# A two-layer streaming encoder step on one core: values by channel, decays broadcast per token, another order of D's heads, an earlier first sum of squares

## What is computed

```python
h = rms(x, lp['norm_mix']); proj = h @ lp['w_in']
# group C, per head; dmat is a fixed causal decay
att = jnp.einsum('bihd,bjhd->bhij', qc, kc) * dmat
y = jnp.einsum('bhij,bjhe->bihe', att, vc) + jnp.einsum('bihd,bhde->bihe', qc, S) * cross
# group D, per head; bh are summed forget gates, igh input gates, m_t a running maximum
dm = jnp.where(tril, bh[..., :, None] - bh[..., None, :] + igh[..., None, :], -jnp.inf)
sc = jnp.einsum('bthd,bshd->bhts', qc, kc) * jnp.exp(dm - m_t[..., None])
num = jnp.einsum('bhts,bshe->bhte', sc, vc) + g[..., None] * jnp.einsum('bthd,bhed->bhte', qc, C)
# group B
q = rms(q_lat, lp['mla_q_norm']) @ lp['mla_wq_b']
kv = concat(past_ckv, ckv_new) @ lp['mla_wkv_b']
```

## Time and profile before

| | us |
|---|---|
| runs: median of 3 (least, most) | 972.83 (969.71, 972.98) |
| the profiled execution | 973.24 |
| its span, first to last instruction | 971.5 |
| TensorE busy with matmuls | 957.7 |
| VectorE, GpSimd, ScalarE busy | 505.5, 398.6, 201.1 |
| mean granted TensorE clock | 0.995 |

### The profile page before, as it was taken

How to read it: one execution, slowest core, us unless ns; L and a number is a source line. 1 busy time by engine, 2 the same in 40 slices (tenths; PEclk the granted TensorE clock), 3 DMA queues, 4 the chain that set the end, 5 groups by cost and what they waited for, 6 DMA issues and landing times. The chain is left out here.

```text
span 971.5 us, 15085 instructions
## 1 busy us (share of the span) xinstructions
PE 957.7 (99%) x5875; PEld 848.5 (87%) x5875; DVE 505.5 (52%) x989; ACT 201.1 (21%) x440; POOL 398.6 (41%) x386
## 2 busy tenths in 40 slices
PE   7999999999999999999999999999999999999998
PEld 6777887776999999999967678877779999999998
DVE  5464446773756556512253545568465665654321
ACT  3123233623000110100031142344320010001001
POOL 8000110033866666576301003001267666666770
PEclk9999999999999999999999999999999999999999
DMA  9932211117644554343433321121174554434421
GB/s 251 271 106 87 90 47 45 48 45 166 176 131 138 152 145 131 120 144 128 135 111 98 106 66 50 44 87 48 14 206 133 148 149 136 131 122 138 144 93 39
DMA packets 159043, 112.14 MB, mean 115 GB/s; under 512 B 10102, under 2 KB 156956, under 8 KB 158844
## 3 DMA queue, kind: packets, MB, share of 16 engines
q1 hardware_dynamic: 154388, 104.50, 37.3%
q0 software_dynamic: 3952, 5.92, 2.2%
q10 hardware_dynamic: 632, 0.75, 0.3%
HBM read 108.89 MB, written 2.27 MB: 114 GB/s over the span
## 5 line engine op out<-in xcount | busy, mean ns | idle before, releaser
L728 PE MATMUL ps<-hT,ring 128*128 128x320 f32 x576 | 164.3, 442 | 0.1
L728 PEld LDWEIGHTS ps<-hT,ring 128*128 128x128 f32 x576 | 109.5, 193 | 47.3 <-issue 3.8
L599 POOL TENSOR_TENSOR work<-ring 128x512 f32<-128x512 f32 (+1 forms) x66 | 82.5, 1250 | 153.3 <-issue 117.6
L1076 PE MATMUL ps<-mixT,ring 128*128 128x160 f32 x672 | 105.0, 299 | 0.0
L1076 PE MATMUL ps<-hT,ring 128*128 128x160 f32 x672 | 98.7, 300 | 1.3 <-DVE hT L1959 1.3
L1076 PE MATMUL ps<-hT,work 128*128 128x160 f32 x672 | 98.5, 299 | 0.0
L1076 PEld LDWEIGHTS ps<-mixT,ring 128*128 128x128 f32 x672 | 95.8, 190 | 0.0
L1076 PEld LDWEIGHTS ps<-hT,ring 128*128 128x128 f32 x672 | 93.7, 190 | 2.0 <-DVE hT L1959 1.5
L1076 PEld LDWEIGHTS ps<-hT,work 128*128 128x128 f32 x672 | 93.6, 190 | 0.1
L600 POOL TENSOR_TENSOR ring<-ring 128x512 f32<-128x512 f32 (+1 forms) x66 | 83.3, 1262 | 5.2
L601 POOL TENSOR_TENSOR work<-ring 128x512 f32<-128x512 f32 (+1 forms) x66 | 83.0, 1257 | 5.2
(11 more groups left out here) (380 smaller groups left out, 1466.1 us busy)
## 6 DMA issues: line engine op xcount, KB each, us to landing
ring<-in_w_gu SPq DMA_DIRECT2D x88, 512.0 KB, 5.2
ring<-in_w_in SPq DMA_DIRECT2D x44, 512.0 KB, 4.8
ring<-in_w_down SPq DMA_DIRECT2D x32, 512.0 KB, 4.5
ring<-in_w_out SPq DMA_DIRECT2D x16, 512.0 KB, 4.1
ring<-in_w_down SPq DMA_DIRECT2D x16, 384.0 KB, 3.7
cst<-in_consts POOLq DMA_DIRECT2D x1, 1664.0 KB, 11.9
ring<-in_w_in SPq DMA_DIRECT2D x2, 640.0 KB, 7.6
wqb<-in_mla_wq_b POOLq DMA_DIRECT2D x2, 384.0 KB, 7.6
```

Of the source, the lines that this page charges most:

```text
L599: step(tt(s3, a11, a21, ALU.subtract))
L728: ins = mm(bank(use, 0, T, m), w[:, k, c:c + m], hT[:, k, 0:T], start=(k == 0), stop=(k == KT - 1))
L1076: ins = mm(bank(use, at * HT, HT), left, right(k), start=(opens and k == 0 and at == 0), stop=(closes and k == n - 1), skip_group_check=True)
```

## The change

- The values of C and D are projected by channel with `feature`, two tiles of 128 channels each. ScalarE copies each to wt (columns 0 to 319 of two halves, `value_raw`), TensorE turns it in three transposes per tile (`value_tiles`), and ScalarE copies the result to vaug.
- The query squares of the two latent tiles are added by VectorE first, so that qms takes three products instead of six. Of gx, four products of one column become one of four columns, over a small diagonal that VectorE makes.
- dd is one product of all 320 columns; VectorE adds the mask in three pieces that pick the columns of the former layout.
- The order of D's heads: rq1, rk0 and rk1 come ahead of the scores and decays of the next head instead of behind them, and VectorE makes the next head's dmx after the weights of this one.
- Layer 0's first sum of squares: GpSimd's pair adds go; TensorE multiplies each square tile, the first three between the two halves of x's transposes. The cached latents move behind ql0 and ql1, on TensorE, ScalarE and VectorE.
- Layer 1: the squares and copies of ql0 and ql1 are interleaved with the key tiles.
- GpSimd's second weight mix of a layer waits for h_sums (before, the third did). Clears of wt cover columns 320 to 575 (before, 512 to 575).

```diff
@@ the dense uses of PSUM, two banks in turn
-    d(..., "mfg", "mv0", "mv1", "mv2")
-    u += [("cnT", (4,)), ("qms", (5,)), ("qt0", (6,)), ("qt1", (7,)), ("qt2", (2,))]
+    d(..., "mfg", "mv0", "mv1")
+    u += [("cnT", (4,)), ("qms", (5,))]
+    d("mvt0", "mvt1")
+    u += [("qt0", (6,)), ("qt1", (7,)), ("qt2", (2,))]
-    fill = [("rv1", "rv2"), ("rqs0", "lx0", "rqs1"), ("rks0", "lx1", "rks1"), ("rg0",)]
+    fill = [("rv1",), ("rqs0", "lx0", "rqs1", "rvt0", "rvt1"), ("rks0", "lx1", "rks1"), ("rg0",)]
@@ GpSimd
-                if i == 2:
+                if i == 1:
                     need(pool, "h_sums", l, 4)
...
-                    for n in range(3):
-                        pool.wait_ge(sem("squared"), 2 * n + 2)
-                        step(nc.gpsimd.tensor_tensor(hT[:, 2 * n, 0:T], hT[:, 2 * n, 0:T], hT[:, 2 * n + 1, 0:T], ALU.add),
-                             "sq_pairs")
                     pool.dma_start(cst[:, 2 * P:c1], I["consts"][:, 2 * P:c1]).then_inc(sem("consts_loaded"), 16)
...
-                                   (wt[:, :, 512:576], 0.0), ...
+                                   (wt[:, :, T:576], 0.0), ...
@@ TensorE, start
+            def turn_x(ks): ...
+            def first_sum(ks):
+                for k in ks:
+                    need(pe, "squared", 0, 2 * KT, k + 1)
+                    ins = mm(bank("ms1", 0, T), C("ones"), hT[:, k, 0:T], start=(k == 0), stop=(k == KT - 1), ...)
+            turn_x(range(0, KT // 2))
+            claim(pe, "ms1", 0)
+            first_sum(range(0, 3))
+            turn_x(range(KT // 2, KT))
+            fill(first_sum(range(3, KT)), "ms1")
@@ in place of tokens()
+            def value_tiles(which, l, p):
+                u = f"{which}t{p}"
+                claim(pe, u, l)
+                need(pe, "v_raw", l, 4, (0 if which == "mv" else 2) + p + 1)
+                if which == "rv":
+                    need(pe, "wt_pad", l, 1)
+                for t in range(NT):
+                    ins = nc.tensor.transpose(bank(u, t * P, P), wt[:, p, t * P:(t + 1) * P], ident)
+                fill(ins, u)
@@ TensorE, in the layer
                 if l == 0:
-                    past_latents()
-                    norm_sum("ms1", l)
...
-                if l == 0:
-                    need(pe, "past_T", l, 1)
-                    latents_out(PAST_TILES)
-                else:
+                if l > 0:
                     past_latents()
...
                     feature(f"ql{p}", l, "ql", p * P, P, wait_h=(p == 0))
                 if l == 0:
+                    past_latents()
+                    need(pe, "past_T", l, 1)
+                    latents_out(PAST_TILES)
...
-                for t in range(NT):
-                    tokens(f"mv{t}", l, "mv", 0, G, t)
+                for p in range(2):
+                    feature(f"mv{p}", l, "mv", p * P, P)
...
                 for t in range(NT):
-                    for p in range(2):
-                        ins = mm(bank("qms", t, 1), qls[:, p, ...], C("ones")[:, 0:1], start=(p == 0), stop=(p == 1))
+                    ins = mm(bank("qms", t, 1), qls[:, 0, ...], C("ones")[:, 0:1], start=True, stop=True)
                 fill(ins, "qms")
+                for p in range(2):
+                    value_tiles("mv", l, p)
...
-                for h in range(H):
-                    mm(bank("gx", h, 1), C("headrow", H)[:, h * P:(h + 1) * P], r3[:, DEC - 1:DEC], ...)
+                mm(bank("gx", 0, H), C("ones", H), r3[:, DEC:DEC + H], start=True, stop=True)
...
-                    mm(bank(u, 0, 256), sel, r2[:, 0:256], start=True, stop=True)
-                    mm(bank(u, 256, 192), sel, r2[:, 128:320], start=True, stop=True)
-                    fill(mm(bank(u, 448, 64), sel, r2[:, 256:320], start=True, stop=True), u)
+                    fill(mm(bank(u, 0, T), sel, r2[:, :], start=True, stop=True), u)
...
                     if h + 1 < H:
-                        d_scores(h + 1)
                         u, name, p = (("rq1", "rq", 1), ("rk0", "rk", 0), ("rk1", "rk", 1))[h]
                         feature(u, l, name, p * P, P)
+                        d_scores(h + 1)
@@ ScalarE
+                def value_raw(u, p):
+                    wait_filled(act, u, l)
+                    step(A(wt[:, p, 0:T], bank(u, 0, T), ACT.Copy), "v_raw")
+                    now_read(act, u)
+                def value_copy(which, grp, p):
+                    u = f"{which}t{p}"
+                    wait_filled(act, u, l)
+                    step(A(vaug[:, :, 2 * p:2 * p + 2, 0:HD], bank(u, 0, NT * P)..., ACT.Copy), f"vaug_{grp}")
+                    now_read(act, u)
...
                 keys_copy(0)
-                value_copy(0)
+                wait_filled(act, f"do{H - 1}", l)
+                value_raw("rv0", 0)
                 keys_copy(1)
                 exponentials(0)
...
-                value_copy(1)
-                value_copy(2)
+                value_raw("rv1", 1)
                 probs_copy(0)
                 exponentials(1)
                 keys_copy(2)
                 conv_input(0)
+                for p in range(2):
+                    value_copy("rv", "c", p)
                 probs_copy(1)
@@ VectorE
+                if l > 0:
+                    key_copies(PAST_TILES[0:2], 0)
+                query_latents(0)
+                if l > 0:
+                    key_copies(PAST_TILES[2:], 2)
+                query_latents(1)
+                if l == 0:
+                    key_copies(PAST_TILES, 0)
...
-                    step(v.tensor_tensor(dmx[:, :], bank(f"dd{h}", 0, 512), C("negmask"), ALU.add), "dmx")
+                    for a, q0, n in ((0, 0, 256), (256, 128, 192), (448, 256, 64)):
+                        step(v.tensor_tensor(dmx[:, a:a + n], bank(f"dd{h}", q0, n), C("negmask")[:, a:a + n], ALU.add),
+                             "dmx" if a == 448 else None)
...
                     need(dve, "decay_d", l, H, h + 1)
-                    if h + 1 < H:
-                        decay_arg(h + 1)
                     wait_filled(dve, f"ds{h}", l)
                     step(v.tensor_tensor(wt[:, h % 2, 0:512], bank(f"ds{h}", 0, 512), dh[:, h % 2, :], ALU.mult))
                     now_read(dve, f"ds{h}")
                     step(tails(h, dh[:, h % 2, :], HD + 1), "w_d")
+                    if h + 1 < H:
+                        decay_arg(h + 1)
                     if h > 0:
                         d_out(h - 1)
                 d_values(H - 1)
+                step(v.memset(wt[:, :, T:TP], 0.0), "wt_pad")
```

More of the change, by code:

```diff
@@ L190 @@
 NCH = len(CHUNKS)
-LAST_USE = {"kvr": "kvr", "ql": "ql1", "mo": "mo1", "mv": "mv2", "mq": "mq1", "mk": "mk1", "rq": "rq1",
-            "rk": "rk1", "rg": "rg1", "rv": "rv2", "lx": "lx1", "lg": "lg1"}
+LAST_USE = {"kvr": "kvr", "ql": "ql1", "mo": "mo1", "mv": "mv1", "mq": "mq1", "mk": "mk1", "rq": "rq1",
+            "rk": "rk1", "rg": "rg1", "rv": "rv1", "lx": "lx1", "lg": "lg1"}
 LAST_USE.update({f"o{i}": f"o{2 * i + 1}" for i in range(4)})
@@ L729, in feature @@
                 fill(ins, use)
[L731 to L735, removed]
-                for k in range(KT):
-                    ins = mm(bank(use, 0, n), hT[:, k, t * P:(t + 1) * P], w[:, k, c:c + n],
-                             start=(k == 0), stop=(k == KT - 1))
-                fill(ins, use)
+            def value_tiles(which, l, p):
[4 more added lines that the diff above has]
+                    need(pe, "wt_pad", l, 1)
+                for t in range(NT):
+                    ins = nc.tensor.transpose(bank(u, t * P, P), wt[:, p, t * P:(t + 1) * P], ident)
+                fill(ins, u)
             def key_tiles(use, l, ready, n):
@@ L857, in _ @@
                 claim(pe, "qms", l)
-                need(pe, "qlat_sq", l, 2)
                 need(pe, "qlat", l, 2)
                 for t in range(NT):
-                    for p in range(2):
-                        ins = mm(bank("qms", t, 1), qls[:, p, t * P:(t + 1) * P], C("ones")[:, 0:1],
-                                 start=(p == 0), stop=(p == 1))
+                    ins = mm(bank("qms", t, 1), qls[:, 0, t * P:(t + 1) * P], C("ones")[:, 0:1], start=True, stop=True)
                 fill(ins, "qms")
+                for p in range(2):
+                    value_tiles("mv", l, p)
                 for t in range(NT):
@@ L936, in between @@
                     if h == 0:
-                        for t in range(1, NT):
-                            tokens(f"rv{t}", l, "rv", 0, G, t)
+                        feature("rv1", l, "rv", P, P)
                     elif h == 1:
@@ L1271, in key_stats, with latent_squares @@
                         step(A(ksq[:, :, :], kv[:, :, 0:HD], ACT.Square), "k_squared")
+                def latent_squares(p):
+                    wait_filled(act, f"ql{p}", l)
+                    step(A(qls[:, p, 0:T], bank(f"ql{p}", 0, T), ACT.Square), "qlat_sq")
                 need(act, "arena_b", l, 1)
[L1274 to L1280 removed]
```

(11 more changed lines are left out.)

88 lines of the change are left out of this document (41 added, 47 removed).

## The result

The changed kernel takes 979.04 us, the median of five executions (978.48 to 980.99), where the kernel before takes 972.83 beside it: a ratio of 1.0078 with an interval of 1.0062 to 1.0093. It is slower by 0.8%, clearly more than the 0.5% that I took for the border, and the forecast of 968 (963.5 to 972) missed in size and in sign. POOL is the profile's name for GpSimd.

What follows compares the result with a forecast made beforehand. TensorE, busy nearly throughout and slowed in places by its clock, was taken as the bound. Savings less new waits summed to -5.1 us: 973.24 - 5.1 - 0.4 = 967.7, say 968, range 963.5 to 972.

Steps and rivals of the forecast that it cites:

- The start: First layer's start: new order +0.8 us, earlier 680 KB load and late landings +0.7; together +1.5 (bounds -0.5 and +3.5).
- rival (d): First layer's start: constants' load delays first chunk and rows, each microsecond beyond 16 adding one; 973.5 at 22; 7%.
- The last head: Last head of D: TensorE waits 2.7 us a layer for VectorE's weights (+5.4); clock then falls (+2.6).
- Rival (a): Last head of D: the wait comes but the clock doesn't fall behind it; 965.4 us; 25%.
- Clock at rq1: Projection rq1 in D: reordered heads keep the clock at 2.4 GHz; 1.7 us a layer, -3.4 in all.
- rival (b): Projection rq1 in D: the clock still falls, so the reorder fails its purpose; 970.4 us; 9%.
- Units of dd: Group D: one product of 320 columns saves 0.52 us in each of eight units; -4.2 us (bounds 3.8 and 4.6).
- Values by channel, query squares and gx: Values of C and D by channel -4.0 us, with +0.9 of waits; query squares -1.3; gx -1.4.
- Head 0's wait: First head of D: full speed uncovers VectorE, so TensorE waits 0.5 us a layer, +1.0 in all.
- The mix: Second weight mix, now after h_sums: TensorE's wait of 1.3 us for hT goes, with 0.1 in layer 0; -1.4.
- Rival (e): Four places of transposes: they pull the clock down, 1.7 us each, 6.8 in all; 974.8 us; 4%.
- Rival (c): Last head of D: no wait, as VectorE and ScalarE are done sooner than summed; 960 us; 4%.

Runs made afterwards that it cites:

- late constants: Changed kernel with GpSimd waiting for six squares before issuing the 680 KB of constants and the loads behind it; 971.77 us, ratio 1.0005.
- the cover: Changed kernel with late constants, and projection rk1 again behind ds3 and dd3; 960.97 us, ratio 0.9890.

## Why the prediction was wrong

**The start: the step that failed.** The paragraph on the first layer's start moved one load of 680 KB, rightly from 12.6 to 7.4 us, and gave its landing 0.7 us. But POOL's queue had 17 loads behind it that moved along, and I costed none. The profiles split the 11.9 us: 7.7 for the 16 small loads and the large one behind them (of which at most 2.5 the large one, and 2 what this execution is longer than another), 0.8 for the 680 KB, 2.9 for the rows behind the chunk (33.98 less 31.09), which even late constants leave and which the earlier sum of squares uncovers, and 0.5 for the new order itself. The profile of the late constants is a long one; with a kvr at 32.0, as in another, the 680 KB get 2.8 and the rows 0.9. I had listed the price of this case as rival (d), with its point at a landing of 21 us, and given it 7%. The rows landed at 23.7. Its reason against, small loads ahead of the constants on the queue, looked at the wrong side of them. The rate, one microsecond for each behind 16, was too low as well, since it gives 7.7 us for 23.7: with a wait of 8.4 us came the low clock, and the first two projections took 3 us longer for it. The new order itself was put at 0.8.

**The last head: mechanism right, size off.** Wait (2.8 for 2.7) and chain (4.16 for 4.15) came as summed from the earlier trace rows. The clock's fall behind it was put at 1.3 us a layer with a bound of 1.7. It is 3.2 in layer 0 and 1.8 in layer 1 of the changed kernel (147.18 and 145.84, less 141.22 with the cover and 2.8 of wait), and 2.6 a layer by the medians with late constants. The stretch at the lower level is some 6.5 us long in layer 0 and 3.4 in layer 1 (3.7 us at a mean of 0.55); the four of the earlier trace rows, from which I took the bound, are no upper limit. Rival (a), no fall, is refuted in all five runs that have this wait, in both layers.

**Clock at rq1.** It came back, as forecast (-3.4), and rival (b) is refuted. The reason I gave, that the run of four-row products is parted by a projection, fits the run with three dd products, but the projection is not needed: one dd product without the reorder came with it too. And what it is worth is less than rq1's 1.7 us. At full speed head 0's weights are late by 0.30 us in the old order, and D gained 1.15.

**Units of dd.** 0.52 us each was an optimistic end: the four-row product of 320 columns costs 0.73 from start to start, more than the 0.55 of a projection product, where the sum had let it run at their pace. Why it doesn't, the rows don't tell. Eight units give 3.0 instead of 4.2 us, under my bound of 3.8.

**Right.** Values by channel, query squares and gx: -5.1 for -4.7 from kvr to ds0, and with the cover the stage from group B's first key tiles to the last output products is 114.58 for 115.13 in each layer, 0.55 less, as forecast (1.0 less 0.45; the wait itself is 0.30). Head 0's wait 0.43 for 0.5, with some luck: the terms as written give 0.4 (6.4 less 6.0), and the dd unit in them was too short. No wait at kvr of layer 1: -1.0 for -0.8. The mix: -2.1 for -1.4. Rival (e), transposes that pull the clock down, is refuted at all four places: 1.00 at 67 to 76, 158 to 162, 541 to 551 and 630 to 634. As in the earlier trace rows, what the Trainium skill ("TensorE: Matmul & The Clock Gate", Part 4: PE-mode transpose) says of transposes does not show here. The test is a mild one: transposes fill at most 1.8 of the four microseconds from 158, and other products stand on both sides.

**Rival (c)**, no wait at the last head, is refuted by the wait of 2.8 us.

## What to carry to other kernels

When a wait goes from a queue, list every instruction behind it that moves forward, not the first one alone, and ask of each transfer what it will share the engines with in its new place. A piece of work used as filler is cover for somebody: before moving it from behind a step, look for the step's last consumer and sum its chain; here one projection on the wrong side of ds3 cost 5.4 us a layer. And a slow clock can hide a wait: what comes back with the clock is bounded by the next engine that is late.

## What the hardware showed beyond expectation

- Two DMA queues with work got the engines packet by packet, not byte by byte: 159 packets against 161 in 2 us, while their shares were 77% and 27%. With POOL's loads early, the second half of the first weight chunk landed at 22.0 us where it had landed at 15.3.
- The idle of 2.8 us ahead of the last head_out came with the lower clock in all five runs that had it, in both layers; idles of 0.43 and 1.46 us in the same group came with it in none. It cost about as much as the idle itself. The length of an idle alone doesn't tell: at the start, one of 2.4 us in the run of before with the early 680 KB came without a fall.
- The clock does or doesn't fall at the same place with the same products ahead of it: rq1 of layer 0 took 6.26 us in the profile of before and 4.58 in that of before with one load of POOL moved.
